# Token-major projections in two 512-row pieces with 512-column products, and a new PSUM bank plan around them

## The reference, cut to what matters

```python
# first block, memory cross attention (256 memory tokens)
k, v = jnp.split(mem @ w_xkv, 2, axis=-1)            # v is "xv": 256 x 1024
o = jnp.einsum('bhsm,bmhd->bshd', pr, v)
# second block
hq, hf, hi, hg, sq, sk, sv = jnp.split(u @ w_in, splits, axis=-1)
# hi is "hv" (256 x 512), the value of hgrn2_mix; sv (256 x 512) that of stick_breaking_mix
```

## Time and profile before

| | us |
|---|---|
| median of 3 runs | 1046.16 |
| lowest, highest | 1044.53, 1046.44 |
| the profiled execution | 1045.14 |
| its span on the core | 1043.3 |
| PE busy in the span | 987.7 (95%) |
| DVE busy | 626.1 (60%) |
| ACT busy | 514.7 (49%) |

### The profile page before, as it was taken

One profiled execution on the slowest core, in us unless ns is written; L12 is line 12 of the kernel. 1 busy time (PEld: TensorE's weight loads), 2 busy tenths in 40 slices (PEclk: granted clock), 3 DMA queues, 4 the chain that ended last, 5 costly groups with the idle time before them and its releaser, 6 DMA issues.

```text
span 1043.3 us, 19398 instructions
## 1 busy us (share of the span) xinstructions
PE 987.7 (95%) x8558; PEld 913.2 (88%) x8558; DVE 626.1 (60%) x833; ACT 514.7 (49%) x693; POOL 19.7 (2%) x23
## 2 busy tenths in 40 slices
PE   7999999999999999999996777799999999999998
PEld 6999999899989999998674454499999999999998
DVE  6798789868676874444110110089984765555566
ACT  5576588844675573533111111178657555434453
POOL 0000021001000000000000000000000000000000
PEclk9999999999999999999998988899999999999999
DMA  7665453446235367798999999964421366555531
GB/s 291 243 238 181 189 188 136 158 166 232 92 128 212 146 220 270 314 358 344 422 420 421 419 421 421 420 223 162 162 82 43 130 242 242 168 196 202 198 126 41
DMA packets 34871, 241.74 MB, mean 232 GB/s; under 512 B 4064, under 2 KB 4448, under 8 KB 6368
## 3 DMA queue, kind: packets, MB, share of 16 engines
q1 hardware_dynamic: 33264, 233.32, 58.8%
q0 software_dynamic: 1232, 6.99, 1.8%
q10 hardware_dynamic: 288, 0.15, 0.1%
HBM read 239.36 MB, written 1.08 MB: 230 GB/s over the span
## 4 chain that ended last, share of the span: by engine, by line
PE 76%; DMA 12%; DVE 7%; ACT 2%; SPq 2%; issue 1%; DVEq 0%; ACTq 0%
PE ps L477 19%; PE ps L487 18%; PE ps L488 18%; DMA wr<-in_c_weights 8%; PE ps L561 3%; PE ps L1267 3%; DMA T8b<-in_c_weights 3%; SPq L3042 2%; DVE wlo L2033 2%; PE ps L956 1%; PE ps L1217 1%; DVE xs L2265 1%; ACT whi L1377 1%; PE ps L1294 1%; PE ps L520 1%
## 5 line engine op out<-in xcount | busy, mean ns | idle before, releaser
L2033 DVE TENSOR_TENSOR wlo<-raw,whi 128x2048 fp32r<-128x2048 f32 (+1 forms) x119 | 271.2, 2282 | 112.7 <-ACT whi L1377 112.3
L477 PE MATMUL ps<-XUh,whi 128*128 128x256 f32 x987 | 277.9, 282 | 0.7 <-DVE wlo L2033 0.6
L487 PE MATMUL ps<-XUl,whi 128*128 128x256 f32 x992 | 275.2, 277 | 0.0
L488 PE MATMUL ps<-XUh,wlo 128*128 128x256 f32 x992 | 274.9, 277 | 0.0
L1377 ACT ACTIVATE whi<-raw 128x2048 fp32r<-128x2048 f32 (+1 forms) x119 | 225.1, 1895 | 45.3 <-PE ps L488 38.7
L477 PEld LDWEIGHTS ps<-XUh,whi 128*128 128x128 f32 x987 | 185.8, 188 | 2.8 <-issue 1.7
L487 PEld LDWEIGHTS ps<-XUl,whi 128*128 128x128 f32 x992 | 186.4, 188 | 0.8 <-issue 0.5
L488 PEld LDWEIGHTS ps<-XUh,wlo 128*128 128x128 f32 x992 | 186.4, 188 | 0.0
L2965 DVE SCALAR_TENSOR_TENSOR sphs<-sphs,wsl,ps 128x256 f32<-128x256 f32 x8 | 3.8, 481 | 90.6 <-ACT sphs L1998 71.8
L477 PE MATMUL ps<-ffnah,whi 128*128 128x256 f32 x176 | 48.6, 276 | 0.0
L487 PE MATMUL ps<-ffnal,whi 128*128 128x256 f32 x176 | 48.6, 276 | 0.0
(11 more groups left out here) (636 smaller groups left out, 2371.7 us busy)
## 6 DMA issues: line engine op xcount, KB each, us to landing
raw<-in_c_weights SPq DMA_DIRECT2D x137, 1024.0 KB, 4.9
wr<-in_c_weights SPq DMA_DIRECT2D x36, 1024.0 KB, 26.1
xhi<-in_c_weights SPq DMA_DIRECT2D x12, 1024.0 KB, 26.4
xlo<-in_c_weights SPq DMA_DIRECT2D x12, 1024.0 KB, 26.4
extra<-in_c_weights SPq DMA_DIRECT2D x10, 1024.0 KB, 27.8
T<-in_c_weights SPq DMA_DIRECT2D x5, 1024.0 KB, 26.1
T8b<-in_c_weights SPq DMA_DIRECT2D x5, 1024.0 KB, 26.4
acb<-sums POOLq DMA_DIRECT2D x4, 1024.0 KB, 5.0
```

The lines of the kernel that those rows point to most:

```text
L477: pe.matmul(ps, h, x, start=start, stop=False, skip_group_check=loose)
L487: pe.matmul(ps, h(k), xl(k), start=False, stop=False, skip_group_check=loose)
L488: t = pe.matmul(ps, l(k), xh(k), start=False, stop=stop and k == kt - 1, skip_group_check=loose)
L2033: dve.tensor_tensor(l[:, 0:n], r, h[:, 0:n].bitcast(F32), ALU.subtract).then_inc(*did("w_lo", "split", i))
```

## The change

1. The weights of xv, hv and sv are packed by `halved`: a piece is 512 rows by 512 columns, still 1 MB; two pieces (upper and lower rows) make one block of 512 output columns.
2. `chunk_tok` streams 512 columns a matmul: 2 tiles x 4 row blocks x 3 = 24 a piece. Each token tile has a bank of its own, `(name, c // 2, j)`; both are taken at the even piece and accumulate over both pieces. The cut in xv 0 is gone.
3. xv is evicted after every second piece, each tile's 512 columns by one ACT copy.
4. In the second stretch `chunk_tok` uses banks 6 and 7 alone, and the scores, z and rem turn among banks 0 to 5. sk, hg, `stick_out`, `hgrn_out` and the sums still turn among all eight.
5. On ACT hv is evicted once, behind `level(4)` and ahead of `soft_z(0)`, with two copies of 512 columns; sv once, behind `stick_a(0)`.

```diff
+    def halved(name, w, c0, n):
+        for c in range(c0, c0 + n, 512):
+            for k in (0, 512):
+                add(name, w[k:k + 512], slice(c, c + 512))
...
+        def chunk_tok(name, c, xh, xl, banks=bank, among=(0, 1, 2, 3, 4, 5, 6, 7)):
             i = first[name] + c
             h, l = split_of(i)
-            ps, free = banks.take(name, c)
-            w.wait_ge(*free)
+            if c % 2 == 0:
+                for j in range(2):
+                    _, free = banks.take(name, c // 2, j, among=among)
+                    w.wait_ge(*free)
             w.wait_ge(*at_("split", i))
+            k0 = 4 * (c % 2)
             for j in range(2):
-                t = triple(ps[:, 256 * j:256 * j + 256], lambda k: xh[:, k, 128 * j:128 * j + 128], lambda k: xl[:, k, 128 * j:128 * j + 128],
-                           lambda k: h[:, k, :], lambda k: l[:, k, :], kt, ready, cut=cut and j == 0)
+                f = slice(128 * j, 128 * j + 128)
+                t = triple(banks.ps(name, c // 2, j)[:, :], lambda k: xh[:, k0 + k, f], lambda k: xl[:, k0 + k, f],
+                           lambda k: h[:, k, :], lambda k: l[:, k, :], 4, start=k0 == 0, stop=k0 == 4)
...
-                ps, free = ebank.take("hsc", lv, j)
+                ps, free = ebank.take("hsc", lv, j, among=(0, 1, 2, 3, 4, 5))
...
-                ps, free = ebank.take("sz", hd)
+                ps, free = ebank.take("sz", hd, among=(0, 1, 2, 3, 4, 5))
...
-                ps, free = ebank.take("srem", hd)
+                ps, free = ebank.take("srem", hd, among=(0, 1, 2, 3, 4, 5))
...
-        chunk_tok("hv", 0, XUh, XUl, 8, None, banks=ebank)
+        chunk_tok("hv", 0, XUh, XUl, banks=ebank, among=(6, 7))
...
         for c in range(4):
             upcoming("xv", c)
-            w.wait_ge(*at_("used", first["xv"] + c))
-            copy(v2[:, :, 256 * c:256 * c + 256], halves(bank.ps("xv", c))).then_inc(*bank.emptied("xv", c))
+            if c % 2:
+                w.wait_ge(*at_("used", first["xv"] + c))
+                for j in range(2):
+                    copy(v2[:, j, 256 * c - 256:256 * c + 256], bank.ps("xv", c // 2, j)[:, :]).then_inc(*bank.emptied("xv", c // 2, j))
...
         level(3)
-        tokens("hv", hv, 0)
         ahead(first["sv"] + 1, end)
         level(4)
+        tokens("hv", hv)
         soft_z(0)
         level(5)
-        tokens("hv", hv, 1)
         ahead(first["hg"], end)
         soft_z(1)
-        tokens("sv", sv, 0)
         level(6)
         ahead(first["hg"] + 1, end)
         stick_a(0)
-        tokens("sv", sv, 1)
+        tokens("sv", sv)
         level(7)
```

More of the change, by code:

```diff
@@ L207, in weights @@
     several("xq", I["w_xq"][0], 0, 1024)
-    several("xv", I["w_xkv"][0], 1024, 1024)
+    halved("xv", I["w_xkv"][0], 1024, 1024)
     several("xo", I["w_xo"][0], 0, 1024)
@@ L218, in weights @@
     several("sk", w2, 2560, 512)
-    several("hv", w2, 1024, 512)
-    several("sv", w2, 3072, 512)
+    halved("hv", w2, 1024, 512)
+    halved("sv", w2, 3072, 512)
     several("hg", w2, 1536, 512)
@@ L525, in chunks_late @@
                         between()
-        def chunk_tok(name, c, xh, xl, kt, ready, banks=bank, cut=False):
+        def chunk_tok(name, c, xh, xl, banks=bank, among=(0, 1, 2, 3, 4, 5, 6, 7)):
             i = first[name] + c
             h, l = split_of(i)
-            ps, free = banks.take(name, c)
-            w.wait_ge(*free)
+            if c % 2 == 0:
+                for j in range(2):
+                    _, free = banks.take(name, c // 2, j, among=among)
+                    w.wait_ge(*free)
             w.wait_ge(*at_("split", i))
+            k0 = 4 * (c % 2)
             for j in range(2):
-                t = triple(ps[:, 256 * j:256 * j + 256], lambda k: xh[:, k, 128 * j:128 * j + 128], lambda k: xl[:, k, 128 * j:128 * j + 128],
-                           lambda k: h[:, k, :], lambda k: l[:, k, :], kt, ready, cut=cut and j == 0)
+                f = slice(128 * j, 128 * j + 128)
+                t = triple(banks.ps(name, c // 2, j)[:, :], lambda k: xh[:, k0 + k, f], lambda k: xl[:, k0 + k, f],
+                           lambda k: h[:, k, :], lambda k: l[:, k, :], 4, start=k0 == 0, stop=k0 == 4)
             t.then_inc(*did("w_used", "used", i))
@@ L824, in pe_program @@
         for c in range(3):
-            chunk_tok("xv", c, MMh, MMl, 8, None, cut=c == 0)
+            chunk_tok("xv", c, MMh, MMl)
         for mj in range(2):
@@ L834, in pe_program @@
                 t.then_inc(*did("xa_pe", "xa_pT", mj, r))
-        chunk_tok("xv", 3, MMh, MMl, 8, None)
+        chunk_tok("xv", 3, MMh, MMl)
         for hd in range(4):
@@ L839, in pe_program @@
             w.wait_ge(*at_("emptied", "xpT", 1, 1))
-            w.wait_ge(*at_("emptied", "xv", hd))
+            w.wait_ge(*at_("emptied", "xv", hd // 2, 0))
+            w.wait_ge(*at_("emptied", "xv", hd // 2, 1))
             for e in range(2):
@@ L944, in hgrn_scores @@
             if lv == 7:
-                ps, free = ebank.take("hsc", lv)
+                ps, free = ebank.take("hsc", lv, among=(0, 1, 2, 3, 4, 5))
                 w.wait_ge(*free)
@@ L973, in hgrn_out @@
                 w.wait_ge(*at_("emptied", "hsc", 7))
-                w.wait_ge(*at_("emptied", "hv", 1))
+                w.wait_ge(*at_("emptied", "hv", 0, 0))
+                w.wait_ge(*at_("emptied", "hv", 0, 1))
                 for r in range(2):
@@ L1008, in stick_out @@
             w.wait_ge(*at_("sb", "a", g))
-            w.wait_ge(*at_("emptied", "sv", 1))
+            w.wait_ge(*at_("emptied", "sv", 0, 0))
+            w.wait_ge(*at_("emptied", "sv", 0, 1))
             for hl in range(4):
@@ L1031, in pe_program @@
         hgrn_scores(1)
-        chunk_tok("hv", 0, XUh, XUl, 8, None, banks=ebank)
+        chunk_tok("hv", 0, XUh, XUl, banks=ebank, among=(6, 7))
         hgrn_scores(2)
         stick_z(0)
-        chunk_tok("hv", 1, XUh, XUl, 8, None, banks=ebank)
+        chunk_tok("hv", 1, XUh, XUl, banks=ebank, among=(6, 7))
         hgrn_scores(3)
         stick_z(1)
-        chunk_tok("sv", 0, XUh, XUl, 8, None, banks=ebank)
+        chunk_tok("sv", 0, XUh, XUl, banks=ebank, among=(6, 7))
         hgrn_scores(4)
         stick_rem(0)
-        chunk_tok("sv", 1, XUh, XUl, 8, None, banks=ebank)
+        chunk_tok("sv", 1, XUh, XUl, banks=ebank, among=(6, 7))
         hgrn_scores(5)
@@ L1825, in level, with tokens @@
             act.activation(Xs[lv % 2][:, :, :], Xs[lv % 2][:, :, :], ACT.Exp).then_inc(*did("hg_act", "hg", "x_exp", lv))
-        def tokens(name, dst, c):
-            w.wait_ge(*at_("used", first[name] + c))
+        def tokens(name, dst):
+            w.wait_ge(*at_("used", first[name] + 1))
             w.wait_ge(*at_("emptied", "rcol"))
             for j in range(2):
-                t = copy(dst[:, j, 256 * c:256 * c + 256], ebank.ps(name, c)[:, 256 * j:256 * j + 256], scale=rcol[:, j:j + 1])
-            t.then_inc(*ebank.emptied(name, c))
+                copy(dst[:, j, :], ebank.ps(name, 0, j)[:, :], scale=rcol[:, j:j + 1]).then_inc(*ebank.emptied(name, 0, j))
         def soft_z(g):
```

## The result

| | before | after |
|---|---|---|
| median, us (6 runs each) | 1045.8 | 1052.41 |
| lowest to highest | 1044.53 to 1046.44 | 1051.3 to 1057.42 |
| ratio, 95% interval | | 1.0075, 1.0064 to 1.0086 |
| profiled execution; its span | 1045.14; 1043.3 | 1051.86; 1050.1 |

What follows compares the result with a forecast made beforehand. The prediction took PE as the bound (95% busy), with DVE also full in the second stretch and the DMA bounding the experts. It summed -1.9 (xv) + 2.9 (hg 0's start) = +1.0 onto 1045.6: 1046.6 us, range 1044.2 to 1049.2.

Steps and rivals of the forecast that it cites:

- Part 1: Value products: a 512-column matmul takes 0.216 us (upper bound 0.235), a piece 5.28 us, 0.46 less.
- the score line: Float32 score products, 256 columns in two passes, 32 starts, 0.216 us each; taken as nearest to the new 512-column form.
- the trace agrees at 216: Skill formula against trace: 216 ns agrees at 512 columns; at 256 the formula's 109 is contradicted by 117.6.
- Part 2: xv: four pieces take 21.1 us instead of 23.0, PE gains 1.9 (bounds 0 and 2.2), and paired evictions cost nothing.
- I take the whole: From xv through the experts: the whole 1.9 us that PE gains survives the DMA-bound experts.
- the full run begins, and ends, as much earlier as PE does: Experts: PE's work releases the last full DMA run, so it shifts earlier with PE; the whole 1.9 us is kept.
- xv's gain is lost in the experts: Slower rival: some load of the full DMA run isn't released by PE; sum +2.9, 1048.5 us; chance 0.06.
- Part 3: Second stretch up to hv: PE waits 1.07 us within scores 0 for bank 1; hv 1 ends 0.15 late.
- Part 4: hv's eviction on ACT: two copies ahead of `soft_z(0)` make its end 2.35 us later and DVE 1.2 late at `stick_sp`.
- Part 5: Ring of six banks: PE waits 1 us at scores 6; hg 0 starts 1.8 to 2.95 us late, 2.9 taken.
- the fourth rival: 512-column product no faster, 0.235 us a matmul: xv gains 0, hg 0 is 3.8 us late, 1049.4 us; chance 0.06.
- The clock rival: At hg 0: clock falls after a wait between 2.6 and 4.16 us, half of 3.4 us lost, 1048.3 us; chance 0.17.

Runs made afterwards that it cites:

- e3: The changed kernel with only hg 0 moved, to PSUM banks 6 and 7: ratio 1.0044 to the kernel before, median 1048.71 us.
- e4: The changed kernel with eight constant products keeping PE busy in its wait before hg 0: ratio 1.0071 to the kernel before, median 1052.09 us.
- e11: The changed kernel with hv evicted behind `soft_z(0)` and nothing else: ratio 1.0075 to the kernel before, three runs of 1052.39 to 1053.35 us.
- e9: Kernel before with new hv and sv, old xv; hg 0 in bank 6, last scores in 7, first in 4 and 5, hv evicted behind `soft_z(0)`: 1.0019, 1046.74 us.
- e10: Changed kernel with hg 0 in bank 6, last scores in 7, first in 4 and 5, hv evicted behind `soft_z(0)`, 49 constant products in the experts: 1.0039.
- e14: Changed kernel with hg 0 in bank 6, last scores in 7, first in 4 and 5, hv evicted behind `soft_z(0)`: 1.0059, runs 1047.9 to 1053.3 us.

## Why the prediction was wrong, point by point

**Part 1, the product: the term was mis-sized.** 0.216 us was taken, 0.229 measured; the upper bound was 0.235. A piece saves 0.15 us and not 0.46. I had taken the score line for a row of the same kind, and it isn't: L821 issues 16 matmuls and the row has 32 starts, two for each, so a float32 matmul of 256 columns takes 0.43 us, and no row shows how its columns are spread over the two.

Nor is it true that this type with 512 columns is missing from the trace of the kernel before. Another value product (`kv_b`, L722) already makes the tokens stationary and streams 512 columns through the same `triple`. Its rows:

```profile
259.81 0.39 PE L487 MATMUL ps<-wlo,XCh 128*128 128x512 f32 x1
...
262.10 0.39 PE L488 MATMUL ps<-whi,XCl 128*128 128x512 f32 x1
```

Ten steps in 2.29 us are 0.229 us each, the measured size to the last digit. With it the prediction's own working gives 0.6 us for xv and hg 0 late by about 3.5 (2.95, and 0.6 that hv 0 and hv 1 then don't give back), an estimate of +2.9 instead of +1.0: slower, and still too little. Two starts of 256 columns take 2 x 0.1176 in xv, hv and sv, so only 0.006 us a pair was there to be saved; with the shorter step, 2 x 0.1133 (21.75 us for 192), it would be nothing. The cost goes almost wholly with the columns, not with the number of matmuls. The Trainium skill (TensorE: Matmul & The Clock Gate, "Back-to-back issue gap") gives 216 ns at 512 columns by its formula. The prediction's "the trace agrees at 216" was the same misreading, since both traces have 229 there. The 0.2 us that the formula left for xv was nearer to the 0.72 measured than my 1.9, by luck: the formula misses at 256 and at 512.

**Part 2, xv: 0.72 us instead of 1.9, and "I take the whole" failed.** The evictions were free. In the experts the step "the full run begins, and ends, as much earlier as PE does" broke in two. First, the loads: the two `extra` loads were issued at 484.37 instead of 486.31, 1.94 us earlier, but the last T8b landed at 672.07 instead of 672.98, 0.9 earlier. Second, and more, what ends the experts isn't the last landing alone: the products behind it hang on PE's instructions and on its clock, and the tail grew from 3.2 to 5.2 us (part of it scatter, as the six profiles above show). The rival "xv's gain is lost in the experts" came true, with 0.06 for its chance, though by another mechanism than it named: the loads weren't the main thing.

**Part 3, the wait in scores 0: right.** 1.07 forecast, 1.20 measured, same place, same releaser (DVE's read of the diagonal product). hv 1's end was to be 0.15 late; it was 751.46 - 749.70 - 0.74 = 1.0 (the starts of the scores behind it, less the 0.74 by which the whole stretch began late). 1.20 less the 0.15 saved in each of two pieces gives 0.9 of that.

**Part 4, the eviction of hv: mechanism right.** `soft_z(0)` was to be 2.35 late and was 752.82 - 748.70 - 0.74 = 3.4 (the 0.74 is the stretch's own late start); nearly all of the difference is hv 1's lateness of Part 3. `stick_sp` was to be 1.2 late and was 757.37 - 754.43 - 0.74 = 2.2, of which 1.36 shows as DVE's wait.

**Part 5, hg 0: mechanism right, size between.** 2.9 forecast; 781.40 - 776.90 - 0.74 = 3.8 measured. That is to the tenth what the fourth rival had worked out for a product that is no faster, which 0.229 nearly is. DVE's merge began 780.63 - 777.85 - 0.74 = 2.0 late instead of 1.2. The wait at scores 6 (1 us forecast) was 0.38 by its row.

**The clock rival, at 0.17, came true.** It asked for a wait between 2.6 and 4.16 us; the wait was 2.17. At 0.77 over 7.28 us, (1 - 0.77) x 7.28 / 0.5 = 3.3 us were at the lower level, and half of that, 1.7 us, was lost. The rival's price was right; its condition, a wait longer than 2.6 us, was not. e3 and e4 show it from both sides. A wait of 1.47 in e11 did not bring it, 2.08 in e9 did, but 2.08 in e10 and e14 did not: no length of a wait alone decides it here.

**The steps that failed.** The product's cost (0.216 for 0.229, Part 1), which carried xv and hg 0 with it; "I take the whole 1.9" across the experts (Part 2), where the last down product came later, not earlier; and the clock behind the wait, which the sum held at nothing.

**The sum.** Forecast: -1.9 + 2.9 = +1.0. Measured in the profiles' spans: xv -0.7, an early start that isn't the change's -1.2, the experts +3.1, the second stretch +5.6 (hg 0's start 3.8, its clock 1.7), the rest 0.1: +6.8 from unrounded numbers. All errors had one sign, and I had treated them as independent: the same row stood behind xv's gain, hv's catching up and hg 0's lateness, so that when it fell, three terms fell, and the longer wait then made the falling clock likely.

## What to carry to other kernels

Before counting on fewer and wider matmuls, ask whether the excess you want to save goes with the matmuls or with the columns; a row of another type or pass count doesn't tell, and one uncertain row that stands behind several terms should widen the range once for each of them. A bank plan is a set of waits: what reads a bank last, and what stands in that engine's queue ahead of the read, decides more than the product that writes it; here one bank for hg 0 was worth 3.9 of 5.6 us. Before calling a cost missing from a trace, look for its form under every name and line: here it stood in a small group of another product. Where a stretch is bound by loads, look also at what the engine does behind the last landing, because time won ahead of the stretch arrives there only if that tail has nothing else to wait for.

## What the runs showed of the hardware that I hadn't expected

- An fp32r matmul with 128 x 128 weights starts 0.229 us behind the one before it at 512 columns, in all 16 profiles (0.230 in some pieces). At 256 columns the step is 0.1133 or 0.1176, for whole pieces at a time, at the same granted clock of 1.00: 0.443 or 0.459 ns a column, where 512 columns have 0.448.
- PE can stand still for 1.4 to 2.6 us at an instruction load while the DMA runs at a share of 1.01, though the load itself takes 1.1 us. Whether it does depends on where the blocks end: 64 PE instructions more, in a kernel otherwise as before, brought a stall of 2.59 us, and 256 more one of 0.86.
- A wait of 2.2 us in a stretch in which PE was otherwise full was followed by the lower clock level within a us (0.77 on average over hg 0), and cost 1.5 to 1.7 us more than the wait itself. A wait of 2.08 us did the same in e9 and not in e10 and e14.
